# Two query tiles processed between the first expert slots, with their high parts in one freed weight slot

## The reference, cut to what matters

```python
def peer_layer(h, w_query, sub_keys, expert_down, expert_up):
    query = (ht @ w_query).reshape(t, PEER_HEADS, 2, PEER_HALF)
    sub_scores = jnp.einsum('thpd,hpkd->thpk', query, sub_keys, ...)
    half_vals, half_idx = lax.top_k(sub_scores, PEER_TOPK)
    cand = half_vals[:, :, 0, :, None] + half_vals[:, :, 1, None, :]
    top_vals, top_pos = lax.top_k(cand, PEER_TOPK)
    experts = i1 * PEER_N_KEYS + i2
    gates = jax.nn.softmax(top_vals, axis=-1)
    ...
        u = expert_down[eb]
        act = jax.nn.gelu(jnp.einsum('td,thkd->thk', xb, u), approximate=False) * gb
        vv = expert_up[eb]
        return jnp.einsum('thk,thkd->td', act, vv)
```

## Time and profile before

| | us |
|---|---|
| median of 3 executions (1645.03 to 1647.06) | 1646.43 |
| profiled execution, device time | 1645.22 |
| its span | 1643.4 |
| DVE busy | 1105.8 (67%) |
| PE busy | 1366.6 (83%) |
| first gather issued | 262.06 |
| first dot (dot 0) starts | 298.88 |
| last dot (dot 255) starts | 971.15 |

### The profile page before, as it was taken

The page is one execution under the profiler, slowest core; times in us unless marked ns, Lnnn a source line. Parts: engine busy times, 40 slices in busy tenths (PEclk is TensorE's granted clock), DMA queues, the critical chain, the costliest instruction groups (busy, mean ns, idle before and its releaser), DMA issues.

```text
span 1643.4 us, 17137 instructions
## 1 busy us (share of the span) xinstructions
PE 1366.6 (83%) x6234; PEld 956.4 (58%) x6234; DVE 1105.8 (67%) x2021; ACT 530.2 (32%) x1024; POOL 380.4 (23%) x329
## 2 busy tenths in 40 slices
PE   6999777777777676877777778978999999899997
PEld 6887657522222222322222337966999877689996
DVE  6575564588888688888455555666765578867554
ACT  1443233322222122222111124542543254534431
POOL 1000001245444344444344410100111033001110
PEclk9999889999999899999999998999999999999999
DMA  9554525699999999999999963324554452355550
GB/s 366 200 205 154 205 77 205 236 421 414 422 422 416 417 414 419 348 423 421 421 422 421 421 281 115 142 77 150 186 200 172 174 176 103 128 180 205 176 183 26
DMA packets 116628, 433.17 MB, mean 264 GB/s; under 512 B 6832, under 2 KB 7088, under 8 KB 83520
## 3 DMA queue, kind: packets, MB, share of 16 engines
q0 software_dynamic: 36864, 268.45, 39.7%
q1 hardware_dynamic: 79392, 162.51, 27.8%
q10 hardware_dynamic: 288, 1.11, 0.2%
HBM read 431.00 MB, written 1.05 MB: 263 GB/s over the span
## 4 chain that ended last, share of the span: by engine, by line
PE 47%; DMA 24%; DVE 20%; ACT 5%; issue 2%; SPq 0%; POOL 0%; DVEq 0%; ACTq 0%; POOLq 0%
PE PS L45 46%; DMA EB<-in_experts,EI 23%; DVE EB L78 5%; DVE WL L75 4%; ACT BIG L24 2%; DVE LNV L63 1%; PE PS L84 1%; DVE GV L75 1%; DVE Y L75 1%; DMA W<-in_w_ada 1%; ACT WH L24 1%; DVE XL L75 1%; DVE X L63 1%; ACT EB L24 1%; DVE BIG L63 1%
## 5 line engine op out<-in xcount | busy, mean ns | idle before, releaser
L45 PE MATMUL PS<-EB,BIG 128*128 128x512 f32 x1024 | 490.6, 624 | 167.6 <-ACT BIG L24 167.6
L45 PEld LDWEIGHTS PS<-EB,BIG 128*128 128x128 f32 x1024 | 189.4, 196 | 464.9 <-ACT BIG L24 284.4
L39 POOL DMA_INDIRECT EB<-in_experts,EI x256 | 289.5, 1131 | 607.8 <-PE PS L45 394.2
L78 DVE CUSTOM_DVE_ANT_0 EB<-EB,Y 128x1024 f32<-128x1024 f32 x256 | 313.5, 1225 | 137.5 <-DMA EB<-in_experts,EI 136.5
L75 DVE TENSOR_TENSOR WL<-W,WH 128x1024 fp32r<-128x1024 f32 x240 | 308.6, 1335 | 127.2 <-ACT WH L24 126.7
L24 ACT ACTIVATE WH<-W 128x1024 fp32r<-128x1024 f32 x240 | 237.0, 1048 | 79.8 <-PE PS L45 73.3
L45 PE MATMUL PS<-XH,WH 128*128 128x256 f32 x832 | 241.9, 291 | 12.4 <-DVE WL L75 11.6
L45 PE MATMUL PS<-XH,WL 128*128 128x256 f32 x832 | 235.8, 283 | 0.0
L45 PE MATMUL PS<-XL,WH 128*128 128x256 f32 x832 | 235.7, 283 | 0.0
L24 ACT ACTIVATE BIG<-BIG 128x2 f32<-128x2 f32 (+1 forms) x136 | 31.1, 229 | 444.3 <-DVE BIG L78 443.9
L45 PEld LDWEIGHTS PS<-XH,WH 128*128 128x128 f32 x832 | 160.1, 192 | 15.7 <-DVE WL L75 12.9
(11 more groups left out here) (170 smaller groups left out, 1406.1 us busy)
## 6 DMA issues: line engine op xcount, KB each, us to landing
W<-in_ffn_w SPq DMA_DIRECT2D x32, 2048.0 KB, 8.6
W<-in_w_ada SPq DMA_DIRECT2D x12, 2048.0 KB, 12.4
W<-in_w_in SPq DMA_DIRECT2D x6, 2048.0 KB, 12.7
W<-in_hy_w_in SPq DMA_DIRECT2D x6, 2048.0 KB, 13.5
W<-in_gla_w_in SPq DMA_DIRECT2D x6, 2048.0 KB, 7.9
W<-in_w_query SPq DMA_DIRECT2D x4, 2048.0 KB, 10.3
W<-in_w_out SPq DMA_DIRECT2D x2, 2048.0 KB, 7.8
EB<-in_experts,EI POOLq DMA_INDIRECT x256, 11.2
```

Source lines behind the costliest of these rows:

```text
L39: return lambda e: e.indirect_dma_start(*a, **k)
L45: return lambda e: e.matmul(*a, **k)
L78: return lambda e: e.tensor_tensor_reduce(*a, **k)
```

## The change

The high parts of `wq[2]` and `wq[3]` go to a fourth place, WL[1], which is slot 1, the memory of `wq[1]` itself; they can be written once `wq[1]` is done. WH0 and WH1 are then not needed by them: buffers 4 and 5 are free when `w_out` is done, buffers 6 and 7 when `wq[1]` is done. The last two groups of `wq[1]` move into slots 0 and 2. The splits of `wq[2]` go to slots 6 to 9 and its groups to slots 11, 14, 17 and 20; the splits of `wq[3]` to slots 23 to 26 and its groups to 29, 33, 37 and 41. Since slot 1 is in use until then, `ada[10]` is loaded only when `wq[3]` is done, and `ada[11]`, `hyt[0]` and `g_final`, which come behind it, as well. Eight steps of `choices` run ahead of the loop.

```diff
-        for j, sl, h in ((1, 1, 1), (2, 0, 0), (3, 2, 1)):
+        WH.append(WL[1])
+        for j, sl, h in ((1, 1, 1), (2, 0, 3), (3, 2, 3)):
             wq.append(wplan(A["w_query"], 0, j * 512, sl, h))
         w_ada(10, 1)
+        ada[10].before_w = wq[3]
...
-        queries[2]()
-        queries[3]()
-        for step in query_groups(2):
-            step()
-        later_split(wq[3])
-        drain()
-        queries = query_groups(3)
+        beside = {s: [] for s in range(64)}
+        beside[0].append(queries[2])
+        beside[2].append(queries[3])
+        for s in range(6, 10):
+            beside[s].append(lambda: split_piece(wq[2]))
+        for s, step in zip((11, 14, 17, 20), query_groups(2)):
+            beside[s].append(step)
+        for s in range(23, 27):
+            beside[s].append(lambda: split_piece(wq[3]))
+        for s, step in zip((29, 33, 37, 41), query_groups(3)):
+            beside[s].append(step)
...
-        e_free = {0: (t_wout,), 1: (t_wout,), 2: wq[0].done, 3: wq[0].done, 4: wq[2].done, 5: wq[2].done}
+        e_free = {0: (t_wout,), 1: (t_wout,), 2: wq[0].done, 3: wq[0].done, 4: (t_wout,), 5: (t_wout,)}
...
+        for _ in range(8):
+            next(choice)()
         for s in range(total + LAG):
...
-            if s < 4:
-                tick(2)
-                queries.pop(0)()
-                if s == 3:
-                    e_free[6] = e_free[7] = wq[3].done
-                    t_gf = small(gfin, rows(A["g_final"]), q_done[3])
+            for step in beside.pop(s, ()):
+                step()
+            if s == 2:
+                e_free[6] = e_free[7] = wq[1].done
+                wh_free[wq[2].index] = wq[1].done
+            if s == 41:
+                t_gf = small(gfin, rows(A["g_final"]), q_done[3])
```

More of the change, by code:

```diff
@@ L1238, in build @@
         later_split(wq[1])
-        later_split(wq[2])
         next(query)
@@ L1264, in group @@
                     src = PS[b][:, :].rearrange("p (c t) -> p c t", c=2)
-                    st["q"] = act(lambda e: e.activation(QT[j][:, c:c + 2, :], src, ACT.Copy), tk, *q_free, ordered=False)
+                    st["q"] = act(lambda e: e.activation(QT[j][:, c:c + 2, :], src, ACT.Copy), tk, *((q_done[1],) if j == 3 else t_xt), ordered=False)
                     bank_free[b] = (st["q"],)
@@ L1271, in group @@
                     q_done[j] = st["s"]
-            q_free = (q_done[1],) if j == 3 else t_xt
             return [lambda n=n: group(n) for n in range(4)]
@@ L1458, in build @@
                 split_piece(hyt[0])
-        assert nu == total and chosen and not queries
+        assert nu == total and chosen and not beside
         held[0] = None
```

## The result

The changed kernel takes 1653.51 us (median of 5, 1651.27 to 1653.79) against 1645.53 for the kernel before (median of 5; the 1646.43 further up is that of the first three): ratio 1.0043, 95% interval 1.0033 to 1.0054. It is slower by 0.43%, more than the 0.2% that can be told from no change. That is inside the stated range of 1637 to 1657, and 5.5 us above the stated 1648. The profiled execution took 1651.78, with a span of 1650.0 where it was 1643.4.

The account below looks back on a forecast made before the run. Expert-row DMA bounds the kernel, with DVE equally full. A 17.2 us DMA lead less 18.6 for moved loads gives 1.4 us later (3.3 by idle time), taken as 2; 1645.2 + 2, median 1.2 above: 1648 us, range 1637 to 1657.

Parts of the forecast that it names:

- The bound: From the eighth slice on, expert rows fill the DMA for sixteen slices; DVE is as full in slots 12 to 35.
- the start: First gathers no longer wait: dot 0 at 273.4, gather 6 at 285.2, dot 6 at 293.8, a lead of 28.8 us.
- rival D: At the start, gathers 6 and 7 wait for a group behind up(0), possibly 8 us longer; chance 0.32 together with Rival C.
- Item 1: Before dot 42, eight splits on a full DVE at 1.19 us each lose 9.5 us of the lead.
- Item 2: In slots 7, 9, 23 and 25 the split waits for ACT, 0.6 us each: 2.4 us lost.
- Item 3: Evacuations waiting for PE ahead of a gelu make DVE wait, up to dot 42: 7.3 us lost.
- Rival C: PE falls to its lower clock after waits in slots 14 and 20: 9 us, 1656 us; chance 0.32 together with rival D.
- item 5: DVE's earlier waits for data in dots 6 to 11 and 36 to 41 shrink: 3.9 us won.
- item 4: Early steps shift: steps 18 to 25 leave the slots up to dot 42, 117 to 124 come in: 1.3 us lost.
- The moved loads: Three tile loads and g_final start near 408 in the full stream, 5.8 us a tile: 18.6 us in all.
- A: ACT's evacuations and copies finish before the gelu is wanted, so the stream ends 7.7 us earlier, 1639 us; chance 0.22.
- B: The DMA stays full throughout, only 281 to 286 idle: 18 us won, 1628 us; chance 0.06.

Follow-up runs that it names:

- edit 3: Changed kernel with each of the eight DVE subtractions of wq[2] and wq[3] doubled: 1661.43 us.
- edit 1: Changed kernel with ACT's evacuations of the wq[2] and wq[3] groups, and the scores behind them, moved later by two slots each: 1642.75 us.
- edit 4: Loads of ada[10] and ada[11] cut to an eighth: changed kernel 1642.7 us; control, same cut in the kernel before, 1645.82 us against 1646.64.
- edit 2: Changed kernel with ada[11] ahead of ada[10] in the list of loads: 1645.43 us.
- edit 5: Changed kernel with eight unused 128x256 matmuls behind each up of slots 0 to 13, to keep PE busy: 1656.25 us.

## Why the prediction came out as it did

**The bound and the start held.** The stream's end sets the time, DVE is full in these slots (edit 3), and dot 0, gather 6 and dot 6 came within 0.6 us of the working. The stall behind up(0) in the start, of which rival D made much, is as long as stated.

**Item 1, the splits**, held: 9.5 us stated, doubled they cost 10.0 by the last dots and 7.9 by the medians (edit 3). **Item 2**, the waits of a split for ACT, was stated at 2.4 us and measured 3.1:

```profile
DVE WL L75 <- ACT WL L24: 3.1, 4, 1.1
```

**Item 3 is the term that was mis-sized.** Stated for slots 15, 21 and 35: 1.7, 4.4 and 1.2 us, 7.3 in all. Measured: 5.48, 5.38 and 1.60, 12.5 in all; slot 43 took 3.49 where 4 was stated. The mechanism is shown by edit 1. Most of the difference lies in slot 15. I placed the group of slot 14 behind an up that ran on time, as the earlier trace rows has it, but the group of slot 11 had put PE behind, and PE ran at its lower clock besides. The sentence that waved this away is in the prediction: groups without an evacuation "delay an up by under 3 us" and were priced at nothing. They hold up no evacuation themselves, but they delay the next one. Rival C had a lower clock as a cause, but elsewhere: it let the clock fall behind the waits of slots 14 and 20, as after 5.53 us of pause. There the granted clock was 1.00, from 317 to 361. It had fallen before, and some 2 us of slot 15 are the estimate for that. From 282 it had been 1.00, and after pauses of PE of 1.27 and 2.24 us it read 0.50:

```profile
300.00:304.00 4.00, 2.72 (x4) 0.72 (x3) 2.58 (x6) 2.44 (x4) 0.94 (x1) 0.50 1.01 426
```

Dot 42 came only 1.9 us later than forecast, 406.39 against 404.5, though items 2 and 3 together were 5.9 us short. That is luck in good part. DVE's waits between dots 6 and 42, of the kernel before and then of the changed one:

```profile
DVE EB L78 <- DMA EB<-in_experts,EI: 4.2, 7, 1.2
DVE ST L69 <- ACT LNV L24: 3.3, 2, 1.6
```

```profile
DVE EB L78 <- DMA EB<-in_experts,EI: 1.4, 2, 1.1
DVE ST L69 <- ACT LNV L24: 0.6, 2, 0.3
```

The ST rows are a sum of `choices` that waits for ACT's exp. Together these waits fell from 7.5 to 2.0 us, by 5.5, where item 5 had 3.9. The other 1.6 are a wait that the earlier trace rows show and that no item took as won. The lead at dot 6 was 0.5 us better than stated, and the remaining 2 us or so lie in item 4 and in the short gaps between instructions.

**The moved loads.** That they cost in the full stream what they did not cost before is shown by edit 4 and its control. The price stated was 5.8 us a tile; the dots give 4.8 (edit 2) and 5.0 (edit 4), the medians 6.2 and more. The term held within the measurement.

**The idle time was read with the wrong measure.** The prediction took 23.2 us of idle time from the DMA share; in bytes the same stretch had 58 x (1 - 222/421) = 27.4 us to win. Its second count, by idle time, gave 3.3 us later and the first 1.4, and I took 2. By bytes the loss up to dot 64 is 6.0 and the dots show 5.9. A share that reads 0.97 at 339 GB/s is not a full stream.

**The end of the stream** moved by 4.9 us where 2 were taken. The span grew by 6.6 us and the median by 8.0. Of the span's 6.6, 1.7 us lie between the last dot and the end of the span (673.9 against 672.3). That distance varies from 672.0 to 673.6 in the other profiles, so I put it down to no edit. Its cause, and the rest between span and median, is open.

**Rivals.** A (ACT's order doesn't reach DVE) and B (the DMA stays full) are excluded: edit 1 gained what A said that the waits were worth, and more, and the DMA share was 0.86 from 310 to 320 where B wanted 1.01. C was right that a lower clock costs something, at about a quarter of its price (an estimate, edit 5) and at another place than it said. D's longer stall at the start did not occur. The chance of 0.32 for slower was too low for a sum that was itself on the slower side by 2 us, with its larger unknowns, the waits on PE, all pointing the same way.

## What to carry to other kernels

Work that is slid between the steps of a running pipeline brings its waits along: an instruction that waits for a slow engine should stand in its own engine's queue late enough that it never waits, since everything behind it stops. Moving just that instruction two steps back turned a loss of 0.4% into a gain of 0.2% here. Where a buffer is freed early to start a stream, list what else waited for the same memory; two loads that had been free in the gap came out at 5 us each in the full stream. And measure a transfer-bound stretch by the bytes that it moved, not by the share of time in which its engines were busy.

## What the runs showed of the hardware that I had not expected

Sixteen DMA engines can count as 0.97 busy while they move 339 GB/s, in a stretch that DVE and PE pace; in the full stream a share of 1.00 to 1.02 goes with 414 to 424 GB/s. The cause of the lower rate was not looked for. The granted PE clock read 0.50 in a stretch in which PE was busy 2.72 of 4 us, with no pause above 2.3 us since the clock had last risen, near 282; small matmuls in the pauses kept it at 1.00 (edit 5) and cost more time on PE than they gave back.
